# Small operands of VectorE's routing steps: in a PSUM bank instead of SBUF

## The reference, cut to what matters

```
v1, i1 = lax.top_k(s1, 16)           # scores against 128 keys, first half
v2, i2 = lax.top_k(s2, 16)           # second half
cand = (v1[..., :, None] + v2[..., None, :]).reshape(128, 8, 256)
top_s, top_c = lax.top_k(cand, 16)
e1 = jnp.take_along_axis(i1, top_c // 16, axis=-1)
e2 = jnp.take_along_axis(i2, top_c % 16, axis=-1)
expert = e1 * 128 + e2
g = softmax(top_s)
act = gelu(einsum('thkd,td->thk', u_tab[expert], ht))
y = einsum('thk,thkd->td', g * act, v_tab[expert])
```

## Time and profile before

| | |
|---|---|
| median of 3 runs | 1755.15 us (1752.37 to 1760.42) |
| profiled execution | 1748.41 us, span 1746.6 us |
| TensorE busy | 1612.3 us (92%) |
| TensorE weight load busy | 1328.8 us (76%) |
| VectorE busy | 1325.4 us (76%) |
| GpSimd busy | 1025.6 us (59%) |
| ScalarE busy | 721.6 us (41%) |
| mean granted TensorE clock | 0.963 |
| HBM traffic over the span | 248 GB/s |

### The profile page before, as it was taken

One profiled execution on the slowest core, in us unless ns is written; L12 is line 12 of the kernel. 1 busy time (PEld: TensorE's weight loads), 2 busy tenths in 40 slices (PEclk: granted clock), 3 DMA queues, 4 the chain that ended last, 5 costly groups with the idle time before them and its releaser, 6 DMA issues.

```text
span 1746.6 us, 22141 instructions
## 1 busy us (share of the span) xinstructions
PE 1612.3 (92%) x8149; PEld 1328.8 (76%) x8149; DVE 1325.4 (76%) x2045; ACT 721.6 (41%) x1249; POOL 1025.6 (59%) x622
## 2 busy tenths in 40 slices
PE   3899999987899999997799999997999999999994
PEld 1345576733789999997799999996778888888883
DVE  3395477227423999999978888827799999999997
ACT  2002122420324434332599999933233333433331
POOL 1500264002002678785577778867789989899863
PEclk9998969999999999998899999998999999999997
DMA  7766200361411577775689999998999999999971
GB/s 247 275 215 125 26 2 1 95 218 42 145 54 39 184 260 254 262 272 187 214 324 352 368 371 337 365 387 312 376 358 375 385 380 375 368 386 376 370 267 49
DMA packets 221974, 436.55 MB, mean 250 GB/s; under 512 B 40893, under 2 KB 135722, under 8 KB 220330
## 3 DMA queue, kind: packets, MB, share of 16 engines
q1 hardware_dynamic: 178410, 299.85, 49.0%
q0 software_dynamic: 36864, 134.23, 21.2%
q10 hardware_dynamic: 6592, 1.05, 0.4%
HBM read 377.28 MB, written 56.62 MB: 248 GB/s over the span
## 4 chain that ended last, share of the span: by engine, by line
PE 28%; DVE 19%; DMA 9%; ACT 7%; issue 3%; SPq 1%; POOL 1%; POOLq 0%; DVEq 0%; ACTq 0%
PE ps L1568 8%; PE ps L1569 8%; PE ps L1570 8%; DMA u_raw<-in_peer_uT 6%; ACT hot1h L1477 3%; DVE junk L1629 2%; ACT stage L1485 2%; DMA a_in<-act_scr 2%; ACT uth L1449 1%; DVE eq L1702 1%; DVE eq L1704 1%; DMA v_raw<-in_peer_v 1%; DVE cand L1666 1%; DVE route L1705 1%; DVE idx L1664 1%
## 5 line engine op out<-in xcount | busy, mean ns | idle before, releaser
L1428 POOL TENSOR_TENSOR utl<-u_raw,uth 128x1024 fp32r<-128x1024 f32 x128 | 317.3, 2481 | 229.5 <-ACT uth L1449 228.5
L1544 PE MATMUL ps<-h2h,uth 128*128 128x384 f32 x1024 | 350.6, 342 | 12.0 <-POOL utl L1428 7.6
L1438 POOL TENSOR_TENSOR vl<-v_raw,vh 128x1024 fp32r<-128x1024 f32 x128 | 312.2, 2440 | 57.0 <-ACT vh L1449 55.1
L1546 PE MATMUL ps<-h2h,utl 128*128 128x384 f32 x1024 | 345.0, 337 | 0.0
L1545 PE MATMUL ps<-h2l,uth 128*128 128x384 f32 x1024 | 344.9, 337 | 0.0
L1568 PE MATMUL ps<-vh,wh 128*128 128x512 f32 x768 | 302.0, 393 | 14.9 <-DVE wl L1753 11.1
L1570 PE MATMUL ps<-vh,wl 128*128 128x512 f32 x768 | 301.2, 392 | 0.0
L1569 PE MATMUL ps<-vl,wh 128*128 128x512 f32 x768 | 301.1, 392 | 0.0
L1748 DVE TENSOR_TENSOR w_f<-a_in,g_in 128x384 f32<-128x384 f32 x128 | 207.7, 1623 | 57.2 <-DMA a_in<-act_scr 56.6
L1449 ACT ACTIVATE vh<-v_raw 128x1024 fp32r<-128x1024 f32 x128 | 135.6, 1059 | 233.2 <-DMA v_raw<-in_peer_v 187.9
L1544 PEld LDWEIGHTS ps<-h2h,uth 128*128 128x128 f32 x1024 | 194.5, 190 | 13.2 <-POOL utl L1428 8.6
(11 more groups left out here) (345 smaller groups left out, 2469.8 us busy)
## 6 DMA issues: line engine op xcount, KB each, us to landing
u_raw<-in_peer_uT SPq DMA_DIRECT2D x128, 512.0 KB
v_raw<-in_peer_v SPq DMA_DIRECT2D x128, 512.0 KB
w_ada<-in_w_ada SPq DMA_DIRECT2D x12, 2048.0 KB, 9.5
act_scr<-acts SPq DMA_DIRECT2D x64, 384.0 KB
g_scr<-stage SPq DMA_DIRECT2D x12, 2048.0 KB
g_in<-g_scr SPq DMA_DIRECT2D x32, 768.0 KB
a_in<-act_scr SPq DMA_DIRECT2D x64, 384.0 KB
w_q<-in_peer_w_query SPq DMA_DIRECT2D x8, 1024.0 KB, 6.9
```

What stands on the lines that cost most here:

```text
L1428: tt(k.utl[b % 3][:, :, :].rearrange(f3), k.u_raw[:, b % 4].rearrange(f3), k.uth[b % 3][:, :, :].bitcast(F32).rearrange(f3), ALU.subtract) ...
L1438: tt(k.vl[:, n % 4], k.v_raw[:, n % 4], k.vh[:, n % 4].bitcast(F32), ALU.subtract).then_inc(k.vl_done, 1)
L1544: mm(o, hi, k.h2h[:, kt, SP:T], start=(kt == 0), stop=False)
L1546: ins = mm(o, lo, k.h2h[:, kt, SP:T], start=False, stop=(kt == DK - 1))
```

## The change

Five small operands of `routing` move from SBUF to PSUM bank 5: `iota16`, `best`, `cab`, `idxf` and `gsum`. `iota16` is copied there once, at the start of the block. `idxf` was f16 for both sides at once; in PSUM it is f32, 128 numbers for one side, and so is cast anew for each side, ahead of the comparison. The `step` that stood at the cast of `idxf` now stands at the mask.

```
+        idxf = ps[:, 5, 0:P].rearrange("p (h c) -> p h c", h=PH)
+        cab = ps[:, 5, P:3 * P].bitcast(U32).rearrange("p (d c) -> p d c", d=2)
+        iota16, best, gsum = ps[:, 5, 3 * P:3 * P + PTOP], ps[:, 5, 3 * P + 16:3 * P + 24], ps[:, 5, 3 * P + 24:3 * P + 32]
...
-            step(v.tensor_copy(k.best[:, :], k.tops[:, :, 0]))
-            tt(tops, tops, k.best[:, :].unsqueeze(2).broadcast_to([P, PH, PTOP]), ALU.subtract).then_inc(k.exp6_in, 1)
+            step(v.tensor_copy(best, k.tops[:, :, 0]))
+            tt(tops, tops, best.unsqueeze(2).broadcast_to([P, PH, PTOP]), ALU.subtract).then_inc(k.exp6_in, 1)
             use_rows(rows[3])
             c = k.topc[:, :, :].rearrange("p h c -> p (h c)")
-            v.tensor_scalar(k.cab[:, 0], c, 4, None, ALU.logical_shift_right)
-            v.tensor_scalar(k.cab[:, 1], c, PTOP - 1, None, ALU.bitwise_and)
-            step(v.tensor_copy(k.idxf[:, :, :, :], k.idx[:, :, :, :]))
-            step(v.tensor_copy(k.cabf[:, :, :], k.cab[:, :, :]))
+            v.tensor_scalar(cab[:, 0], c, 4, None, ALU.logical_shift_right)
+            step(v.tensor_scalar(cab[:, 1], c, PTOP - 1, None, ALU.bitwise_and))
+            step(v.tensor_copy(k.cabf[:, :, :], cab))
             for side in range(2):
                 e3 = k.eq[:, :, :]
                 e4 = e3.rearrange("p (h c) a -> p h c a", h=PH)
+                v.tensor_copy(idxf, k.idx[:, :, side, :])
                 step(tt(e3, k.cabf[:, side].unsqueeze(2).broadcast_to([P, PH * PTOP, PTOP]),
-                        k.iota16[:, :].unsqueeze(1).broadcast_to([P, PH * PTOP, PTOP]), ALU.is_equal))
-                step(tt(e4, e4, k.idxf[:, :, side, :].unsqueeze(2).broadcast_to([P, PH, PTOP, PTOP]), ALU.mult))
+                        iota16.unsqueeze(1).broadcast_to([P, PH * PTOP, PTOP]), ALU.is_equal))
+                step(tt(e4, e4, idxf.unsqueeze(2).broadcast_to([P, PH, PTOP, PTOP]), ALU.mult))
...
-            step(v.tensor_reduce(k.gsum[:, :], tops, AXX, ALU.add))
-            step(v.reciprocal(k.gsum[:, :], k.gsum[:, :]))
+            step(v.tensor_reduce(gsum, tops, AXX, ALU.add))
+            step(v.reciprocal(gsum, gsum))
...
-                     k.gsum[:, :].unsqueeze(2).broadcast_to([P, PH, PTOP]), ALU.mult)
+                     gsum.unsqueeze(2).broadcast_to([P, PH, PTOP]), ALU.mult)
...
+        v.tensor_copy(iota16, k.iota16[:, :])
         topk(0, (0, 0, 0))
```

More of the change, by code:

```diff
@@ L1131, in place_peer @@
     k.idx = k.sb("idx", [P, PH, 2, PTOP], 85, U32)
-    k.idxf = k.sb("idxf", [P, PH, 2, PTOP], 86, F16)
     k.tops = k.sb("tops", [P, PH, PTOP], 87)
     k.topc = k.sb("topc", [P, PH, PTOP], 87.5, U32)
-    k.cab = k.sb("cab", [P, 2, PH * PTOP], 88, U32)
     k.cabf = k.sb("cabf", [P, 2, PH * PTOP], 89)
-    k.gsum = k.sb("gsum", [P, PH], 90)
-    k.best = k.sb("best", [P, PH], 90.125)
     k.route = k.sb("route", [P, TT, 3, PH * PTOP], 174)
```

## The result

The changed kernel takes 1735.43 us in the median of 4 runs (1731.11 to 1738.61), the kernel before 1754.19 us in 4: a ratio of 0.9902 with a 95% interval of 0.9875 to 0.9928. It is faster by 18.8 us, 1.0%; the forecast was 1738.5. The profiled execution took 1735.53 us with a span of 1733.7, which is 12.9 us less than the profiled span before (1746.6): of the two numbers the medians are the surer, since executions of one kernel differ by 8 us and more.

The account below looks back on a forecast made before the run. VectorE, arriving late at the end of the fourth routing, was taken as the bound until 842.75 us. 19.7 - 2.1 - 1 = 16.6 us off 1748.4 gave 1731.8 profiled, 1738.5 for the median; range 1730 to 1750.

Parts of the forecast that it names:

- VectorE's path moves the end one for one: What VectorE saves before TensorE's transposes at 842.75 us shortens the whole kernel equally; all 16.6 us count.
- what follows the piece stays at 904 us: Sign of being right: from the end of the last routing to the kernel's end stays 904 us.
- Rival 2: Gain lost behind the routing, 860 to 1160 us, if bytes hold it: 1747 with half lost, 1755 with all; 12%.
- An operand in PSUM takes the instruction out of the collision: VectorE routing instructions with a PSUM operand no longer sit out GpSimd's subtractions; L1629's steady 1199 to 1222 ns was the evidence.
- Rival 1: Operand place does not matter: routing stalls stay and only costs of 10.6 us come, 1766 us; 3%.
- Stalls removed, 19.7 us: Gains over four routings: copy 1.7, first `cab` 4.2, `cabf` cast 2.9, compare 3.4, gate 5.6, multiply 1.9 us.
- Costs, 2.1 us: Added in routing: 1.9 us for PSUM shifts and index-list casts, 0.15 us for the starting copy; bounds 1 and 3.
- The multiply, 1.9 us better: Eight routing multiplies by the index list: 10.4 us of stalls removed, 8.5 us of speed lost.
- `cand`, 1 us worse: Untouched addition with two SBUF inputs still collides with GpSimd in the routing; 1 us lost, bounds -3.8 and +4.6.
- The eleventh row in time: Tightest ring row, needed at about 675 us with 5 us left for 0.5 MB: no cost, otherwise 1 us.
- TensorE's remaining wait 11 us: After the change TensorE still waits some 11 us for VectorE's last routing, so the whole gain counts.
- Rival 4: `cand` stalls go too, or TensorE's half-clock stretch shortens; capped by TensorE's 22.9 us of waits, 1734 us; 8%.

Follow-up runs that it names:

- after_again: The changed kernel measured once more, unaltered, on the chip of some follow-up runs; 1736.24 us, ratio to before 0.9901.
- extra8: The changed kernel with each routing comparison done twice, eight more VectorE instructions; 1752.12 us, ratio to before 0.9997.
- half: The changed kernel with comparison and multiply done for only half the slots in the three dense groups, a probe; 1719.32 us, ratio to before 0.9803.
- pool_memset: The kernel before with GpSimd's subtraction replaced by a memset in blocks 0 to 61, a probe; 1725.42 us, ratio to before 0.9834.
- small_only: The kernel before with only `best`, `cab` and `gsum` moved to PSUM; 1746.24 us, ratio to before 0.9959.
- big_only: The kernel before with only `iota16` and `idxf` moved to PSUM; 1740.61 us, ratio to before 0.9929.
- list_f32: The kernel before with the index list as f32 instead of f16, still in SBUF; 1762.95 us, ratio to before 1.0061.
- idxf_sbuf: The changed kernel with the index list kept f16 in SBUF and cast once; 1725.78 us, ratio to before 0.9853.
- idxf_late: idxf_sbuf with one memset put ahead to shift its phase against GpSimd; 1725.76 us, ratio to before 0.9866.
- before_late: The kernel before with one memset of 2048 f16 elements ahead of VectorE's first top-k; 1751.9 us, ratio to before 1.0001.

## Why the prediction was right

The direction, the size and the mechanism held: 1738.5 forecast, 1735.43 measured, 16.6 us of gain against 18.8 (and 16.2 in the repeat). How near the two numbers are is in part luck: the forecast started from a median of 1755.15 that a fourth run made 1754.19, and in the profiled executions alone the gain was 12.9 us (14.9 in the repeat). Step by step:

- *VectorE's path moves the end one for one.* Shown, to within some us. Over the kernels the piece and the time move together. Against before: -18.7 gives -16.2 and -18.8, -26.6 gives -27.9, -23.9 gives -25.8, -12.1 gives -11.8, -5.2 gives -6.2, +11.3 gives +11.4. Against after_again: -4.5 gives -7.1, +19.8 gives +15.9. The forecast's sign that what follows the piece stays at 904 us holds only roughly: it was 903.9 before, 908.7 in the changed kernel and 905.0 in its repeat, and lay between 902 and 909 in every profiled execution. Rival 2 (bytes hold the rest) falls with extra8 and half, although the DMA share of that stretch is now 0.96.
- *An operand in PSUM takes the instruction out of the collision.* Shown by the ranges after and by pool_memset, where the only two long executions met the only two subtractions. Rival 1 is out.
- *Stalls removed, 19.7 us.* As a total right: the piece is 18.7 us shorter with 2.0 us of costs, which leaves 20.7, of which 0.7 is `cand` in the routing. As a list of lines it was wrong to read it as parts that stand alone; small_only and big_only show that the parts are worth 6.2 and 11.8 and not 13.3 and 4.7.
- *Costs, 2.1 us.* They were 2.0: 0.26 for the steps ahead of the first comparison, where I had 0.27, and 0.21 for the second cast, plus 0.09 us for the copy at the start, where I had 0.15. What PSUM costs depends on the instruction. The copy to `best` has 174 ns for 171, the reciprocal 216 for 203, the gate 286 for 291 when free. But the shift has 289 for 220, the mask 284 for 218 and the cast to `cabf` 425 for 294, together 1.1 us of the 2.0. So the rule in "VectorE: DVE Perf Modes" of the Trainium skill, 62 cycles more of fixed cost where an instruction reads PSUM and writes SBUF, is not borne out by the gate, the comparison and the multiply here, and the cast has twice as much. The prediction also laid it on all 56 instructions; only 28 of them read PSUM and write SBUF, an estimated 1.8 us by that page and not 3.6.
- *The multiply, 1.9 us better.* The working was right, and the choice in the kernel is still the weak part of the change: list_f32 shows that the 1.06 us come from the type alone, and idxf_sbuf and idxf_late that with the other stalls gone an f16 multiply in SBUF, its stalls included, is shorter (means of 1368 and 1591 ns) than the f32 one in PSUM (2287).
- *`cand`, 1 us worse.* It was 0.7 us better (13.9 for 14.6). With this sign the forecast would have been 1736.8. Its stalls were also sized too small: 4.6 us came from 14.6 us of busy time, in which overlaps are counted once, less 24 full durations. Free, the 24 have 8.9 us of busy time (pool_memset), so the stalls before were 5.7 us.
- *The eleventh row in time.* Yes: VectorE didn't wait for a row in the routing.
- *TensorE's remaining wait 11 us.* It was 9.6.

Rival 4 has the right idea of a cap and the wrong size: half and idxf_sbuf meet it, but at 28.3 us of the piece and not at 22.9 (of which it took 21 without a reason), since it left out the stretches of TensorE at the lower clock, which the prediction itself had put at some 5 us when it placed block 61's end at 815.

Open: why the gate of the kernel before, which started at 767.86 while GpSimd was in a gather, did not run before the subtraction at 768.47. The same happened to a comparison of small_only (755.22, 5.05 us; the subtraction is recorded from 755.70). Others that began beside a gather ran free: a multiply in pool_memset, and in the kernel before a comparison at 750.21, 0.95 us ahead of a subtraction, and a multiply at 763.85, 0.82 ahead of one. Also open is why the stage starts between 552 and 560 us from execution to execution.

## What to carry to other kernels

Where VectorE and GpSimd work at the same time, look at the range of each VectorE line, not at its mean: one with a shortest of 0.3 and a longest of 5.5 us may be waiting for GpSimd inside its own duration; the two timelines side by side tell. One small operand in PSUM ends that. For the arithmetic on two tensors this had no price here (286 ns for 291, 2277 for 2290), for a shift, a mask or a cast it had 0.07 to 0.13 us apiece, and where it needs a wider type the price can be larger than the stall. Take the sum of such stalls as a forecast for the whole group of instructions, never for one line: the stall goes to the next instruction that is exposed. And a wait of TensorE that vanishes wholly gives back its clock as well, some 1.6 us here.

## What the runs showed of the hardware that was not expected

VectorE and GpSimd fall into step. A delay of 0.95 us ahead of everything was gone before the first routing ended, with the same instructions long from there on (the gate of the third routing at 767.89 for 767.86), and the total did not move (before_late).

GpSimd waits for VectorE as well. Its gathers took up to 2833 ns in the routing of the kernel before and at most 1157 in the changed one, with the same shortest and median (939 and 961, 941 and 961). The long gathers of before (1.76 to 2.83 us, four of them) all began while a comparison or multiply with two SBUF inputs ran, and each ended 0.81 to 0.84 us after it: the one from 761.82 to 764.65 lies beside a comparison that ended at 763.81. A gather that began just ahead of such an instruction was not long (750.17 to 751.13, beside the comparison at 750.21).

A MAX8 whose output lies in PSUM, and index and replace instructions that take their list of values from there, run at nearly the speed they have with SBUF (289 to 293 against 280 ns, 284 against 287, and 275 against 283).
